# Three units instead of two in the row-by-row products of a transformer kernel's norm transitions

## The reference, cut to what matters

```python
h = rms_norm(x, norm_w[layer, 0, 0]) * (1.0 + scale) + shift
y = mixer_ab(h, ...)   # or mixer_cd: h @ w_in, attention, @ w_out
x = x + gate * rms_norm(y, norm_w[layer, 0, 1])
h = rms_norm(x, norm_w[layer, 1, 0]) * (1.0 + scale) + shift
y = swiglu(h, ffn_w_in[layer], ffn_w_out[layer])   # (silu(h @ gate) * (h @ up)) @ down
x = x + gate * rms_norm(y, norm_w[layer, 1, 1])
```

## Time and profile before

| | |
|---|---|
| time, median of 3 runs | 1029.87 us (1028.25 to 1030.72) |
| profiled execution, span from first to last instruction | 1029.8 us |
| its own time, beside the span | not listed apart; the span is 0.1 us from the median of the runs |
| PE busy | 987.3 us, 96% |
| PEld busy | 954.4 us, 93% |
| DVE busy | 792.3 us, 77% |
| ACT busy | 559.9 us, 54% |
| granted clock of TensorE, mean | 0.992 |
| moved from and to memory | 227.59 MB |

### The profile page before, as it was taken

The page is one execution under the profiler, slowest core; times in us unless marked ns, Lnnn a source line. Parts: engine busy times, 40 slices in busy tenths (PEclk is TensorE's granted clock), DMA queues, the critical chain, the costliest instruction groups (busy, mean ns, idle before and its releaser), DMA issues. The chain is left out here.

```text
span 1029.8 us, 21353 instructions
## 1 busy us (share of the span) xinstructions
PE 987.3 (96%) x8118; PEld 954.4 (93%) x8118; DVE 792.3 (77%) x1320; ACT 559.9 (54%) x1126; POOL 4.6 (0%) x14
## 2 busy tenths in 40 slices
PE   6999989999999999999999999999999999999996
PEld 5998768999999999989899999998989899999995
DVE  4758996788888777888788888876767857887775
ACT  2435774644444455574554444445657457666763
POOL 0100000000000000000000000000000000000000
PEclk9999999999999999999999999999999999999998
DMA  9995677488888656813558888774722425555431
GB/s 359 348 271 184 246 269 254 168 309 299 306 306 304 247 185 233 304 57 121 186 217 315 300 301 308 282 262 167 248 66 68 155 80 195 200 197 184 183 115 41
DMA packets 62569, 227.59 MB, mean 221 GB/s; under 512 B 7042, under 2 KB 7298, under 8 KB 62244
## 3 DMA queue, kind: packets, MB, share of 16 engines
q1 hardware_dynamic: 61716, 224.02, 60.5%
q0 software_dynamic: 640, 2.10, 0.9%
q10 hardware_dynamic: 144, 0.52, 0.1%
HBM read 225.04 MB, written 1.57 MB: 220 GB/s over the span
## 5 line engine op out<-in xcount | busy, mean ns | idle before, releaser
L1994 PE MATMUL bank<-hH,wH 128*128 128x258 f32 (+1 forms) x1544 | 444.2, 288 | 12.1 <-DVE hL L1343 8.4
L1995 PE MATMUL bank<-hL,wH 128*128 128x258 f32 (+1 forms) x1544 | 438.0, 284 | 0.0
L1996 PE MATMUL bank<-hH,wL 128*128 128x258 f32 (+1 forms) x1544 | 436.3, 283 | 0.0
L1278 DVE TENSOR_TENSOR wL<-raw,wH 128x1024 fp32r<-128x1024 f32 x270 | 327.9, 1220 | 43.9 <-ACT wH L813 42.8
L1994 PEld LDWEIGHTS bank<-hH,wH 128*128 128x128 f32 x1544 | 292.4, 189 | 20.0 <-issue 11.2
L813 ACT ACTIVATE wH<-raw 128x1024 fp32r<-128x1024 f32 x270 | 276.3, 1047 | 46.8 <-DMA raw<-in_weights 25.0
L1996 PEld LDWEIGHTS bank<-hH,wL 128*128 128x128 f32 x1544 | 293.6, 190 | 0.0
L1995 PEld LDWEIGHTS bank<-hL,wH 128*128 128x128 f32 x1544 | 293.1, 190 | 0.4
L1994 PE MATMUL bank<-aH,wH 128*128 128x256 f32 x592 | 169.2, 286 | 3.0 <-DVE wL L1278 3.0
L1996 PE MATMUL bank<-aH,wL 128*128 128x256 f32 x592 | 168.6, 285 | 0.0
L1995 PE MATMUL bank<-aL,wH 128*128 128x256 f32 x592 | 168.5, 285 | 0.0
(11 more groups left out here) (353 smaller groups left out, 1138.6 us busy)
## 6 DMA issues: line engine op xcount, KB each, us to landing
raw<-in_weights SPq DMA_DIRECT2D x270, 512.0 KB, 4.6
modbuf<-in_mod_w SPq DMA_DIRECT2D x69, 512.0 KB, 6.1
modbuf<-in_w_ada SPq DMA_DIRECT2D x36, 512.0 KB, 6.5
strips<-in_mod_w SPq DMA_DIRECT2D x16, 512.0 KB, 7.0
strips<-in_w_ada SPq DMA_DIRECT2D x12, 512.0 KB, 7.0
strips<-bias_table POOLq DMA_DIRECT2D x8, 256.0 KB, 6.8
raw<-in_mod_w SPq DMA_DIRECT2D x2, 512.0 KB, 4.2
otok<-in_mod_w SPq DMA_DIRECT2D x2, 512.0 KB, 9.8
```

The lines of the kernel that those rows point to most:

```text
L1278: V.tensor_tensor(wL[:, slot, :], raw[:, slot, :], wH[:, slot, :].bitcast(F32), ALU.subtract).then_inc(lo_ready[c], 1)
L1994: mm(out, lhs_h, rhs_h, start=start, stop=False, skip_group_check=True)
L1995: mm(out, lhs_h, rhs_l, start=False, stop=False, skip_group_check=True)
L1996: return mm(out, lhs_l, rhs_h, start=False, stop=stop, skip_group_check=True)
```

## The change

In the four transitions that end with a norm, `first_units` takes the place of `first_pair` and multiplies three units row by row. In f0 and f1 the third one is unit 3, the gate of tile 1, which `gate_up(1)` then leaves out; in f0 it goes to bank 1, and the down products of tile 0 wait until tile 1's gate has been read from there. In cd and sb the third one is unit 2, and `project` begins with unit 3. In sb the transposes of unit 0 now stand directly behind the last sum of squares. The transitions to ab and to f2 keep two units. Nothing is changed on the other engines but the bank from which tile 1's gate is read in f0.

```diff
--- before.py
+++ after.py
@@ -469,7 +469,7 @@
 
         def gu_banks(phase, t):
 
-            return (bank[0] if phase == "f0" and t == 0 else bank[4 + t % 2]), bank[7 - t % 2]
+            return (bank[t] if phase == "f0" and t < 2 else bank[4 + t % 2]), bank[7 - t % 2]
 
 
 
@@ -2065,6 +2065,26 @@
                     sum_square(n, 2)
                     sum_square(n, 3)
 
+            def first_units(p0, outs, a):
+
+                n = NORMS.index(f"A{a}")
+                for e in outs:
+                    unit_ready(p0 + e)
+                pe.wait_ge(misc_taken, misc[FIRST_AFTER[a]] + 1)
+                for k in range(KT):
+                    pe.wait_ge(h_ready, KT * a + k + 1)
+                    cols = slice(k * P, (k + 1) * P)
+                    for e, out in outs.items():
+                        slot = (p0 + e) % RING
+                        last = three(out[:, 0:HW], wH[:, slot, cols], wL[:, slot, cols], hH[:, k], hL[:, k],
+                                     k == 0, k == KT - 1)
+                        if k == KT - 1:
+                            last.then_inc(unit_used[(p0 + e) % 3], 1)
+                    if k in (3, 5):
+                        sum_square(n, (k - 3) // 2)
+                sum_square(n, 2)
+                sum_square(n, 3)
+
             FIRST_AFTER = {1: "modS1", 2: "modS2", 3: "modS3", 4: "modS4", 5: "modG4"}
 
             def turn_values(phase, e):
@@ -2168,6 +2188,8 @@
                     if t >= 2:
                         pe.wait_ge(gu_scaled, at(g0 + t - 1, 2))
                     for n, bk in enumerate(gu_banks(phase, t)):
+                        if (t, n) == (1, 0) and phase != "f2":
+                            continue
                         p = base + 3 * t + n
                         unit_ready(p, i)
                         if t == 1 and n == 1:
@@ -2184,6 +2206,8 @@
                     unit_ready(p, i)
                     pe.wait_ge(aL_ready, g0 + t + 1 if i is None else i * 2 + (g0 + t + 1))
                     slot = p % RING
+                    if phase == "f0" and t == 0:
+                        pe.wait_ge(gu_scaled, g0 + 2)
                     for m in range(KT):
                         out = bank[m // 2][:, (m % 2) * S:(m % 2 + 1) * S]
                         last = three(out, wH[:, slot, m * P:(m + 1) * P], wL[:, slot, m * P:(m + 1) * P],
@@ -2192,7 +2216,10 @@
                             last.then_inc(y_ready, 1)
                     last.then_inc(unit_used[p % 3], 1)
 
-                first_pair(base, gu_banks(phase, 0), a, HW)
+                first = dict(enumerate(gu_banks(phase, 0)))
+                if phase != "f2":
+                    first[3] = gu_banks(phase, 1)[0]
+                first_units(base, first, a)
                 gate_up(1)
                 for t in range(2, 4):
                     gate_up(t)
@@ -2501,8 +2528,8 @@
                     pe.wait_ge(proj_done, PROJ0["cd"] + 16)
                     stick_z(0)
                 if e == 0:
-                    first_pair(base, (bank[4], bank[5]), 2, HW)
-                elif e >= 2:
+                    first_units(base, {n: proj_bank("cd", n) for n in range(3)}, 2)
+                elif e >= 3:
                     project("cd", e)
                 turn_values("cd", e - 1)
 
@@ -2655,8 +2682,9 @@
                 last.then_inc(tok_psum, 1)
 
             base = BASE["sb"]
-            first_pair(base, (bank[4], bank[5]), 4, HW)
-            for e in range(2, 8):
+            first_units(base, {n: proj_bank("sb", n) for n in range(3)}, 4)
+            turn_values("sb", 0)
+            for e in range(3, 8):
                 project("sb", e)
                 turn_values("sb", e - 2)
             project("sb", 8)
```

## The result

The changed kernel takes 1040.46 us (median; 1036.3 to 1041.58) beside 1030.3 us for the kernel before (1028.25 to 1032.8). The ratio is 1.0094, with an interval of 1.0067 to 1.0122: slower by 9.7 us, between 6.9 and 12.6. The forecast was 1038.5, or +8.7.

A forecast was written before the change was run, and what follows sets the result against it. TensorE, busy 96% of the span, was taken as the bound. Terms 2.1 + 0.4 + 2.1 + 2.2 = +6.8, plus 1.9 for the clock, gave 1029.8 to 1038.5 us; own range 1037 to 1040, wider range 1034 to 1041.

The forecast's parts named there:

- The gain of 0.72 us ahead of row 2: Each of four transitions: third unit's products for rows 0 and 1 fill 0.72 us of TensorE's 1.17 us idle.
- The delay of the last sum, 2.16: In the four transitions, the last sums of squares come 24 x 0.12 - 0.72 = 2.16 us later.
- f0 and f1, +2.1 each: Transitions to f0 and f1: no slack from last sum to unit 6, so its whole delay comes through, +2.1 us each.
- The waits were to be 1.2 to 1.4 (rstd) and 1.6 (unit 6): In f0 and f1, TensorE waits 1.2 to 1.4 us for rstd and some 1.6 for unit 6's low half.
- cd, +0.4: Transition to cd: 1.6 us of slack; unit 4's scaling ends at 403.0, unit 6 starts at 403.1, not 402.70: +0.4 us.
- sb, +2.2 for the delay: Transition to sb: transposes, unit 3 and VectorE's queue up to unit 9 move back with the sum: +2.2 us.
- The stall was to be 3.5: In sb, TensorE idles about 3.5 us after the last sum, its transposes waiting for the gelu.
- The clock in sb, +1.9: Behind sb's idle the clock falls for 6 us, TensorE is 2.7 us late; 1.9 counted, ends 0 and 2.7.
- DVE's lead over PE: In sb, VectorE runs 0.7 us ahead of TensorE, so 2.0 of 2.7 us reach its queue and unit 9.
- The sum, +8.7: Whole kernel: +6.8 us over four transitions plus 1.9 for sb's clock, 1029.8 to 1038.5; forecast's chance 0.50.
- The first cause given for the clock's not falling in f0 and f1: Stalls of some 1.3 and 1.7 us are under the 2.04 us idle, until 131.36, that left the clock at 1.00.

The follow-up runs named there:

- late sums: Kernel before, two units, last two sums of squares issued 18 products later in f0 and f1: stages 206.25 and 206.27 us, ratio 1.0040.
- short chain: Changed kernel with unit 6 split ahead of the silu in f0 and f1, silu and gelu tables loaded early: ratio 1.0037.
- the stall filled: Kernel before plus three units in sb only, with 14 unread matmuls behind the last sum: stage +2.13 us, ratio 1.0021.
- the transposes moved: Kernel before plus three units in sb only, transposes of unit 0 put behind unit 3: stage +2.20 us, ratio 1.0025.
- sb alone: Kernel before with three units and early transposes in the transition to sb only: stage +4.64 us, ratio 1.0047.

## Why the prediction was right

Its steps, one by one, against the profile of after:

- The gain of 0.72 us ahead of row 2: the idle went from 1.01 to 0.28, 0.73.
- The delay of the last sum, 2.16: measured 2.17.
- f0 and f1, +2.1 each: +2.17 and +2.18. The waits were to be 1.2 to 1.4 (rstd) and 1.6 (unit 6): 1.10 and 1.56. The late sums show that the delay is the cause, the short chain that it works through unit 6. The size was a little low because I let unit 6 start 0.08 us behind the end of its low half (195.15 behind 195.07); it started 0.14 us behind it before and 0.16 us after.
- cd, +0.4: +0.46, with PE waiting 0.92 us for the scaling of unit 4, which came 1.92 us later from cd's first product (22.39 instead of 20.47), where the forecast had 2.16 less 0.2.
- sb, +2.2 for the delay: +2.13 with the stall filled, +2.20 with the transposes moved. The stall was to be 3.5: 3.47.
- The clock in sb, +1.9: 1.5 in the profile of after, 2.5 with sb alone. That it falls was right: it fell in all three profiles with a stall there (two of 3.47 us, one of 2.89). The size was near by luck, since two errors offset each other. I had the low level last 6 us; it lasted some 3.5 us in two profiles and some 7 in one, so in the profile of after PE lost 1.5 us and not 2.7. And I took off 0.7 us for DVE's lead over PE, of which 0.1 shows. In the profile of after (first fence; sb begins at 715.54) the first product behind the low stretch starts at 21.17 and unit 9 at 37.08; with 14 useless products (second fence; sb begins at 709.76) the same two start at 19.62 and 35.60. PE was 1.55 us behind when the clock was back, and still 1.48 at unit 9:

```profile
736.71 0.37 PE L1994 MATMUL bank<-hH,wH 128*128 128x258 f32 x1
...
752.62 0.39 PE L1994 MATMUL bank<-hH,wH 128*128 128x258 f32 x1 [0.84 <-DVE proj L1420]
```

```profile
729.38 0.37 PE L1994 MATMUL bank<-hH,wH 128*128 128x258 f32 x1
...
745.36 0.39 PE L1994 MATMUL bank<-hH,wH 128*128 128x258 f32 x1 [0.94 <-DVE proj L1420]
```

- The sum, +8.7: +8.4 in the stages, +9.7 (6.9 to 12.6) in the times. The median, 1040.46, is above the forecast's own 1037 to 1040 and only 0.5 us inside the range. No term covered what lies ahead of f0, which was 1.1 us longer in this profile.
- The first cause given for the clock's not falling in f0 and f1 was weak. I had argued with the earlier trace rows that a wait of 2.04 us left the clock alone near 131. In the profile of after the lower level began 0.9 us behind the same wait at the same place:

```profile
128.00:132.40 4.40, 2.37 (x23) 1.46 (x21) 4.33 (x9) 4.35 (x16) 0.00 (x0) 1.00 0.77 257
132.40:135.90 3.50, 3.50 (x20) 3.08 (x16) 3.50 (x11) 2.89 (x12) 0.00 (x0) 0.51 0.83 283
```

  In f0 and f1 it did stay at 1.00 in all thirteen profiles, so the conclusion held, but that row did not carry it.

The Trainium skill's advice against idle between bursts ("TensorE: Matmul & The Clock Gate", "Why this matters for your kernels") is borne out by the three profiles of sb (stalls of 3.47, 3.47 and 2.89 us, granted clock near 0.5 in the low stretch), and by the run in which 14 useless products took the idle's place and the clock stayed at 1.00.

What the runs leave open: whether the fall of the clock behind the stall of sb happens in every execution. The times of the changed kernel spread from 1036.3 to 1041.58, and the fastest, at a mean clock of 0.994 where the others have 0.987 to 0.991, may be one without it; there is no trace of it. Why the low level lasts 3.5 us in one profile and 7 in another stays open too.

## What to carry to other kernels

Before work is pulled forward into an engine's idle time, look at what else is in that engine's queue, and what starts from it on the others: here the last two sums of squares, 1.5 us of work on TensorE, were the head of a chain of 6 us, and they were moved back 2.16 us for 0.72 us of filled idle. Put the filler behind the head of the chain, not ahead of it, and shorten the chain first, because until it has slack the filled idle comes back as a wait at its end. When stages have clean marks, compare stage by stage: differences of 0.3 us could be read here, under a spread of 5 us in the total.

## What was not expected of the hardware

- A wait of 2.0 us stands at the same place (near 131) in all thirteen profiles, with the same instructions in front of it. In seven a low stretch of the clock began within 1.5 us of its end (granted clock 0.51 in the profile of after), in six, that of before among them, none did. So the clock's falls differ from run to run, and with them the time, by a few microseconds.
- The idle ahead of a matmul, as the profile gives it, leaves out 0.16 us of a real wait; distances of starts (0.12 us here in a full queue) show it. What the timeline showed without a bracket was a wait of 0.18.
- A useless product of 128 columns in float32 is two records of 0.11 us, 0.22 us in all (24 of them held PE from 722.10 to 727.46), while a product of 258 columns on the split halves, which the DVE rows list as fp32r, is one record, 0.12 us from start to start.
